# Latent attention layers of a four-layer decoder step: what the in-projection starts with moves into the out-projection ahead of it, and latent squares move from the heads stage into the in-projection

## The chip, the cores and the metric

The kernel runs as one launch on one core of a Trainium2 chip. The metric is the device time of one execution in microseconds (us), lower is better. The engines named below are TensorE (PE), VectorE (DVE), ScalarE (ACT), GpSimd (POOL) and SyncE (SP, which issues every DMA here).

## The reference, cut to what matters

Four layers, each `x <- x + W_out(mixer(in_proj(RMSNorm(x))) * silu(gate))`, on 1024 prompt tokens and 8 sample tokens (T = 1032 columns), width 1024. Layers 0 and 3 are latent attention (MLA), layer 1 is HGRN2, layer 2 is RG-LRU. The part of an MLA layer that the change touches:

```
h = rmsnorm(x, norm_g)
cq, ckv, kpe, gate = split(h @ w_in, [384, 640, 672])     # 384 + 256 + 32 + 512 columns
q   = rmsnorm(cq, g_ql) @ w_uq                            # needs the mean square of cq, of each token
ckv = rmsnorm(ckv, g_kv)                                  # needs the mean square of ckv
k_nope, v = split(ckv @ w_ukv)                            # then norms of q and k, rotary part, attention
```

## The kernel before, in words

Activations lie by feature: `c.x` is 128 partitions x 8 blocks (KD) x 1032 tokens, fp32. A projection is done at about fp32 precision as three products of the rounded type fp32r: weights and source are each split into a high part (ACT, a Copy that rounds) and a low part (a subtraction), and the products are hi x hi, hi x lo and lo x hi. One output block of 128 columns is 8 k-blocks x 3 products x 3 token tiles of 344 = 72 matmuls into three PSUM banks. Output blocks alternate between two sets of banks, two weight slots, and two slots each of parts (`w_hi`, `w_lo`). The order on each engine is written by hand; semaphores join the engines, and every stage (`Stage.block`) ends in a barrier of all engines.

`latent_projection` (the in-projection of an MLA layer, nine output blocks and then the narrow `kpe` block) does in this order:

- SP: in layer 0 the eight blocks of `x` and the weights; in layer 3 (`first` is False) `x` is already in place, so the weights alone. Then six small tables (`m.load`, `w_uq` among them), then a weight block whenever a slot is free.
- ACT: the table set for Ln and Exp, `src_hi` of eight blocks (L667), the high parts of weight blocks 0 and 1 (L656), squares of `x` (L659), and later `root()`: Ln and Exp of the sums of squares (L684, L687), which give `rstd`.
- POOL: the low parts of all weight blocks (L705). DVE: `src_lo` (L766), adding up the squares (L773), then `take(n)` (L777), which multiplies block n in PSUM by `rstd` into `m.z`.
- PE: block 0 (L729), each k-block as its `src_lo` comes; in layer 0 then the column sums of the squares (`sums()`, L740) and block 1, in layer 3 block 1 and then the sums; then blocks 2 to 8, each after `take` has emptied its banks.

`mla_heads` starts with squares of the two `ckv` blocks (ACT, L1060) and three `cq` blocks (L1062), a scaling of `w_uq` in place (L1065) and two additions on POOL (L937, L940). PE begins with the column sums of the `ckv` squares (L984), the first query product (L1010), sums of the `cq` squares (L1017) and a turn of `kpe` (L1021); then come, tile by tile of 128 tokens, keys (L1029), values, queries and transposes.

`output_projection` of the RG-LRU layer (layer 2) is `streamed_projection` with a `ring`: PE has blocks 0 and 1 nearly done before the stage starts (L226), the parts of the source are made by then, and blocks 2 to 7 follow (L382); DVE adds each to `c.x` (L461). It has no `norm_layer`, so ACT and POOL only split weights (L315, L351).

Of the kernel before, what the change touches and what calls it, by code (L numbers as in the profile page):

```python
# [66 lines left out]

class Chip:


    def __init__(self, nc, ctx, dram):
# [9 lines left out]
        self.parts = parts[:, :, 0, :], parts[:, :, 1, :]  # L81
        self.ident = sb("ident", [P, P])
# [147 lines left out]
def streamed_projection(c, w, blocks, kt, src, drain, norm_layer=None, early=None, x_back=None, x_in=None, x_out=None, ring=None, clear=False):  # L230
# [7 lines left out]
    with Stage(c, clear=clear) as st:  # L238
# [16 lines left out]
        if norm:  # L255
            norm.bank = base[0]
        block = st.block()
# [3 lines left out]
        def _(sp):  # L261
# [49 lines left out]
        def _(act):  # L311
# [20 lines left out]
            with act.Fori(2, pairs) as i:  # L332
                for u in range(2):
                    weight_hi(2 * i + u, u, 16 * i + (16 - 8 * ready))
                    square(2 * i + (u - 2), u)
            if blocks % 2:
                weight_hi(blocks - 1, 0, 16 * (pairs + 1))
            if norm:
# [9 lines left out]
        def _(pool):  # L348
# [4 lines left out]

            for m in range(ready, 4):
# [3 lines left out]
            with pool.Fori(2, pairs) as i:  # L358
                for u in range(2):
                    weight_lo(2 * i + u, u)  # L360
                    if norm:
                        norm.accumulate(pool, 2 * i + (u - 2), u)
            if blocks % 2:
                weight_lo(blocks - 1, 0)
            if norm:
                norm.accumulate(pool, blocks - 2, 0)

# [47 lines left out]
        def _(dve):  # L415
# [21 lines left out]
            if x_in is None:  # L437
# [21 lines left out]
def output_projection(c, w, kt, src, next_layer, x_back=None, x_in=None, x_out=None, ring=None, clear=False, early=None):  # L459
# [3 lines left out]
                        x_out=x_out, ring=ring, clear=clear, early=early)  # L463
# [127 lines left out]

def latent_projection(c, m, layer, j):
# [3 lines left out]
    with Stage(c) as st:  # L596
# [3 lines left out]
        src_hi = st.sb("src_hi", [P, KD, T], F32R)  # L600
        src_lo = st.sb("src_lo", [P, KD, T], F32R)
# [19 lines left out]
        drained = st.sem("block_drained")  # L621
        if first:
            c.decays.semaphores(st)
        block = st.block()
        pairs = blocks // 2
# [3 lines left out]
        def _(sp):  # L629
            if first:  # L630
                sp.dma_start(c.x[:, 0, :], dram["x"][:, 0, :]).then_inc(x_landed[0], 16)
                sp.dma_start(c.gains[:, :, :], dram["norm_g"]).then_inc(gains_landed, 16)
            sp.dma_start(ws[:, 0, :, :], w[0]).then_inc(w_landed[0], 16)
            for k in range(1, KD if first else 0):
                sp.dma_start(c.x[:, k, :], dram["x"][:, k, :]).then_inc(x_landed[k], 16)
            sp.dma_start(ws[:, 1, :, :], w[1]).then_inc(w_landed[1], 16)
# [6 lines left out]
            with sp.Fori(1, pairs) as i:  # L643
                for u in range(2):
                    sp.wait_ge(w_lo_done, 2 * i + (u - 1))
                    sp.dma_start(ws[:, u, :, :], w[bass.ds(2 * i + u, 1)].rearrange("a p k m -> p (a k) m")) \
                      .then_inc(w_landed[u], 16)
            sp.wait_ge(w_lo_done, blocks - 2)
            sp.dma_start(ws[:, 0, :, :], w[blocks - 1]).then_inc(w_landed[0], 16)

        @block.scalar
        def _(act):
            def weight_hi(n, u, landed_now):
                act.wait_ge(w_landed[u], landed_now)
                wait(act, summed, n - 1)
# [5 lines left out]
            load_ln_exp(nc)  # L661
            if first:
                act.wait_ge(gains_landed, 16)
            for k in range(KD):
# [4 lines left out]
                if k == 1:  # L669
# [2557 lines left out]
```

## Time and profile before

| | us |
|---|---|
| median of 3 runs (lowest, highest) | 2446.91 (2445.93, 2453.77) |
| the profiled execution, its own time | 2443.1 |
| its span, first to last instruction | 2441.3 |
| in-projection of layer 0 | 0 to 138.6 |
| heads stage of layer 0 | 138.6 to 237 |
| out-projection of the RG-LRU layer | 1655.7 to 1735.4 |
| in-projection of layer 3 | 1735.7 to 1867.6 |
| heads stage of layer 3 | from 1867.8 |

Times in the rows below are microseconds from the start of the span. PE is busy in 94% of the span, so the places to look at are those where it is not, and those where its clock is low: PEclk is the clock granted to it as a share of full speed (1.0 is 2.4 GHz, 0.5 is 1.2 GHz).

### The profile page before, as it was taken

The numbers are of one execution on the slowest core, as the hardware profiler recorded it, in microseconds if no ns is written. First come the engines' busy times: TensorE is split into PE (matmuls) and PEld (weight loads), VectorE is DVE, ScalarE is ACT, GpSimd is POOL, SyncE is SP. The second block draws the span as 40 slices with busy tenths as digits, with TensorE's granted clock in tenths as the row PEclk, the third lists the DMA queues.
The fourth block names the chain that finished last, engine by engine and source line by source line (L and its number), as shares of the span: only waits on it lengthen the run. The fifth ranks groups of instructions, "written<-read, shape, count | busy, mean of one in ns | idle before, by whom it ended". The sixth has DMA issues, their size and how long they took to land. (4 is left out here: it accounts for less than half of the span.)

```text
span 2441.3 us, 47634 instructions
## 1 busy us (share of the span) xinstructions
PE 2292.1 (94%) x17886; PEld 1901.0 (78%) x17886; DVE 1252.1 (51%) x1972; ACT 1097.7 (45%) x1873; POOL 722.9 (30%) x809
## 2 busy tenths in 40 slices
PE   7989999999889999999968989989899999999998
PEld 6956666666688999999968989989896566666668
DVE  5133555566443666766674166681412355655552
ACT  4055544555344544455552256661302655545541
POOL 2134322333030222332233325541211532322311
PEclk9999999999999999999979999999999999999999
DMA  4020434434331111111102111101213023434333
GB/s 151 26 75 1 122 107 114 112 95 120 121 130 45 49 51 55 40 50 54 46 28 106 35 53 49 40 20 52 70 35 117 28 83 108 119 102 112 110 105 139
DMA packets 104278, 187.62 MB, mean 77 GB/s; under 512 B 15722, under 2 KB 84332, under 8 KB 102916
## 3 DMA queue, kind: packets, MB, share of 16 engines
q1 hardware_dynamic: 104068, 184.81, 24.6%
q8 instruction: 133, 2.18, 0.4%
q14 instruction: 77, 0.63, 0.1%
HBM read 164.84 MB, written 19.92 MB: 76 GB/s over the span
## 5 line engine op out<-in xcount | busy, mean ns | idle before, releaser
L1507 POOL TENSOR_TENSOR latents_t_lo<-pages_t,latents_t_hi 128x256 fp32r<-128x256 f32 x256 | 187.7, 733 | 551.4 <-ACT latents_t_hi L1744 550.7
L1906 DVE TENSOR_REDUCE sums<-w_uq 128x8 f32<-128x512 f32 x256 | 175.2, 684 | 263.1 <-ACT w_uq L1752 262.8
L1752 ACT ACTIVATE w_uq<-ps 128x512 f32<-128x512 f32 x256 | 152.8, 597 | 209.6 <-PE ps L1592 208.8
L2209 PE MATMUL ps<-src_hi,w_hi 128*128 128x344 f32 x720 | 243.3, 338 | 2.8 <-ACT normed L2365 2.6
L1592 PE MATMUL ps<-w_uk_hi,latents_t_hi 128*128 128x512 f32 x512 | 236.1, 461 | 1.0 <-POOL latents_t_lo L1507 1.0
L2209 PE MATMUL ps<-src_hi,w_lo 128*128 128x344 f32 x720 | 233.5, 324 | 0.0
L2209 PE MATMUL ps<-src_lo,w_hi 128*128 128x344 f32 x720 | 233.4, 324 | 0.0
L1592 PE MATMUL ps<-w_uk_lo,latents_t_hi 128*128 128x512 f32 x512 | 203.7, 398 | 0.0
L1592 PE MATMUL ps<-w_uk_hi,latents_t_lo 128*128 128x512 f32 x512 | 203.3, 397 | 0.0
L1761 ACT ACTIVATE latents<-ps,bias,rq 128x256 f32<-128x256 f32 (+7 forms) x128 | 106.1, 829 | 131.3 <-DVE bias L1920 117.5
L1606 PE MATMUL ps<-residual,normed 96*128 96x512 f32 (+3 forms) x384 | 153.6, 509 | 8.8 <-ACT w_uq L1752 6.2
L2511 POOL TENSOR_TENSOR normed<-normed,k 128x512 f32<-128x512 f32 x56 | 96.8, 1730 | 201.4 <-ACT normed L2380 168.4
L2209 PEld LDWEIGHTS ps<-src_hi,w_hi 128*128 128x128 f32 x720 | 139.0, 193 | 7.2 <-ACT normed L2365 3.5
L461 DVE TENSOR_TENSOR residual<-ps,residual 128x1032 f32 (+1 forms) x30 | 37.0, 1233 | 206.8 <-PE ps L382 201.6
L2209 PEld LDWEIGHTS ps<-src_lo,w_hi 128*128 128x128 f32 x720 | 138.9, 193 | 0.5
L2209 PEld LDWEIGHTS ps<-src_hi,w_lo 128*128 128x128 f32 x720 | 138.4, 192 | 0.0
L1592 PEld LDWEIGHTS ps<-w_uk_hi,latents_t_hi 128*128 128x128 f32 x512 | 97.1, 190 | 45.4 <-issue 23.8
L2365 ACT ACTIVATE normed<-ps 128x344 f32<-128x344 f32 x96 | 43.0, 454 | 194.5 <-PE ps L2209 188.6
L729 PE MATMUL ps<-src_hi,w_hi 128*128 128x344 f32 x432 | 94.5, 328 | 29.8 <-POOL w_lo L705 22.4
L351 POOL TENSOR_TENSOR w_lo<-w_slots,w_hi 128x512 fp32r<-128x512 f32 (+1 forms) x24 | 44.2, 1844 | 242.4 <-ACT w_hi L315 242.4
L1592 PEld LDWEIGHTS ps<-w_uk_hi,latents_t_lo 128*128 128x128 f32 x512 | 96.9, 189 | 23.6
L1592 PEld LDWEIGHTS ps<-w_uk_lo,latents_t_hi 128*128 128x128 f32 x512 | 97.7, 191 | 18.9 <-issue 3.8
(368 smaller groups left out, 5582.3 us busy)
## 6 DMA issues: line engine op xcount, KB each, us to landing
pages_t<-in_pages_t SPq DMA_DIRECT2D x256, 208.0 KB, 2.6
pages<-in_pages SPq DMA_DIRECT2D x256, 128.0 KB, 2.1
w_slots<-in_w_hgrn SPq DMA_DIRECT2D x30, 512.0 KB, 3.6
w_slots<-in_w_mla_in SPq DMA_DIRECT2D x18, 512.0 KB, 3.7
x_home<-residual SPq DMA_DIRECT2D x2, 4128.0 KB, 14.5
w_slots<-in_w_rg SPq DMA_DIRECT2D x14, 512.0 KB, 3.5
residual<-in_x SPq DMA_DIRECT2D x8, 516.0 KB, 9.0
residual<-in_x SPq DMA_DIRECT2D x1, 4128.0 KB, 13.8
```

Of the source, the lines that this page charges most:

```text
L351: nc.gpsimd.tensor_tensor(w_lo[:, u, :, :], ws[:, u, :, :], w_hi[:, u, :, :].bitcast(F32), ALU.subtract).then_inc(w_lo_done, 1)
L461: streamed_projection(c, w, KD, kt, src, lambda m, psum: c.nc.vector.tensor_tensor(block_of(c.x, m), psum, block_of(c.x, m), ALU.add), nex ...
L729: mm = nc.tensor.matmul(c.ps[:, NT * u + t, 0:TT], a[:, u, k, :], b[:, k, cols], start=(k == 0 and p == 0), stop=(k == KD - 1 and p == 2))
L1507: nc.gpsimd.tensor_tensor(lat_lo[:, g % DEPTH, :, :].rearrange("p k t -> p (k t)"), ring[:, g % RING, 0:KVL], lat_hi[:, g % DEPTH, :, :].r ...
L1592: mm = nc.tensor.matmul(keys(g), x[:, e, k, :], y[:, k, :], start=(n == 0), stop=(n == len(products) - 1))
L1606: mm = nc.tensor.matmul(S[:, lo:hi], c.h[0:QK, 2 * f + e, qt * P:(qt + 1) * P], c.x[0:QK, 2 * f + e, lo:hi], start=True, stop=True)
L1752: nc.scalar.activation(sq[:, g % 2, :], keys(g), ACT.Square).then_inc(squared, 1)
L1761: nc.scalar.activation(probs[:, G % 2, e, 0:n], S[:, 0:n], ACT.Exp, scale=m.rq[:, qt, 2 * f + e:2 * f + e + 1], bias=bias[:, u:u + 1], acc ...
L1906: nc.vector.tensor_reduce(ss[:, b % 2, p, :], sq[:, g % 2, :].rearrange("p (h d) -> p h d", h=H), AX.X, ALU.add).then_inc(ssum, 1)
L2209: mm = nc.tensor.matmul(bank[:, 0:TT], w[:, slot, kk, :], x[:, kk, cols], start=(kk == 0 and m == 0), stop=(kk == KD - 1 and m == 2))
L2365: nc.scalar.activation(raw[:, place, t * TT:(t + 1) * TT], bank[:, 0:TT], ACT.Copy) \
L2511: nc.gpsimd.tensor_tensor(halves(z[:, l % 2, 0:SEQ], half)[:, :, 0, :], halves(dd[:, l % 2, 0:SEQ], half)[:, :, 0, :], halves(k[:, 0:SEQ], ...
```

## The change

Four edits.

1. In the RG-LRU out-projection (`carry`), ACT makes the high part of each block of the new `x` times the gain of layer 3, and its square; POOL adds the squares up; DVE makes the low part; all for blocks 0 to 6. The first weight block of layer 3 is loaded and split there too. The new buffer `carried_src` lies at the top of the on-chip memory; the rest uses free parts of `c.h`. ACT's, POOL's and DVE's loops are written out there.
2. `latent_projection` of layer 3 starts with block 0 at once (k-blocks 0 to 6 from what was carried), makes only block 7's parts and square, and does the sums right after block 0 in place of after block 1.
3. `latent_projection` of layer 0 sums blocks 0 and 1 together, k-block by k-block (`FIRST_TWO`), with the column sums after both. Loads come in another order, DVE makes the low parts of the first two weight blocks, `load_ln_exp` moves behind the squares, and the high part of weight block 2 stands behind `root()` and the high part of the `kpe` weights.
4. In both, ACT squares the latents (blocks 0 to 4) between weight blocks, POOL adds those of `cq`, ACT scales `w_uq`; `mla_heads` no longer does any of it. All engines' loops over blocks are written out.

```diff
 class Carried:            # in Chip: self.carried = Carried(self, parts)
+        self.hi, self.lo = src[:, 0, :, :], src[:, 1, :, :]     # carried_src [P, 2, KD, T], F32R
+        self.sums = c.h[:, 0, :]
+        self.squares = c.h[:, 1, :], c.h[:, 7, :]
 ...
 def streamed_projection(..., carry=None):                      # SP
+            if carry is not None:
+                sp.dma_start(cd.w, carry[1]).then_inc(w_next_landed, 16)
 ...                                                            # ACT, in square(m, u)
+                if carry is not None:
+                    act.wait_ge(drained, m + 1)
+                    nc.scalar.activation(cd.hi[:, m, :], c.x[:, m, :], ACT.Copy,
+                                         scale=c.gains[:, carry[0], m:m + 1]).then_inc(next_hi, 1)
+                    if m >= 2:
+                        act.wait_ge(next_added, m - 1)
+                    nc.scalar.activation(cd.squares[u], c.x[:, m, :], ACT.Square).then_inc(next_squared, 1)
 ...
+                for m in range(4, blocks):
+                    weight_hi(m, m % 2, 16 * (m // 2) + (16 - 8 * ready))
+                    square(m - 2, m % 2)
 ...
+            if carry is not None:
+                act.wait_ge(w_next_landed, 16)
+                nc.scalar.activation(cd.w_hi, cd.w, ACT.Copy).then_inc(w_next_hi, 1)
+                square(blocks - 2, 0)
 ...                                                            # DVE
+            if carry is not None:
+                one(0, 0)
+                one(1, 1)
+                for m in range(2, blocks):
+                    one(m, m % 2)
+                    next_low(m - 2)
+                next_low(blocks - 2)
 ...
 def latent_projection(c, m, layer, j):                         # SP
             if first:
-                sp.dma_start(c.x[:, 0, :], dram["x"][:, 0, :]).then_inc(x_landed[0], 16)
                 sp.dma_start(c.gains[:, :, :], dram["norm_g"]).then_inc(gains_landed, 16)
-            sp.dma_start(ws[:, 0, :, :], w[0]).then_inc(w_landed[0], 16)
+                sp.dma_start(ws[:, 0, :, :], w[0]).then_inc(w_landed[0], 16)
+                for k in range(2):
+                    sp.dma_start(c.x[:, k, :], dram["x"][:, k, :]).then_inc(x_landed[k], 16)
+            sp.dma_start(ws[:, 1, :, :], w[1]).then_inc(w_landed[1], 16)
+            if not first:
+                sp.dma_start(ws[:, 0, :, :], w[2]).then_inc(w_landed[0], 16)
 ...                                                            # ACT
             if first:
+                weight_hi(0)
+                act.wait_ge(gains_landed, 16)
+                for k in range(KD):
+                    high(k)
+                    if k == 1:
+                        weight_hi(1)
+                    square(k)
+                load_ln_exp(nc)
                 c.decays.exponentials(act)
                 root()
+                keys_hi()
+            else:
+                high(KD - 1)
+                square(KD - 1)
+                weight_hi(1)
+                load_ln_exp(nc)
                 root()
+                weight_hi(2)
+                keys_hi()
+            for n in range(2 + less, blocks):                  # less = 0 if first else 1
+                weight_hi(n)
+                if n >= 4:
+                    latent_square(n - 4)
+                if n - 4 == NQL - 1:
+                    for k in range(NQL):
+                        nc.scalar.activation(m.wuq[:, k, :], m.wuq[:, k, :], ACT.Copy, scale=m.gql[:, k:k + 1])
 ...                                                            # POOL
+            for n in range(2 if first else 1, blocks):
+                weight_lo(n)
 ...
+                if 5 <= n < 4 + NQL:
+                    add_latent_squares(n - 4)
 ...                                                            # PE
-            one(0, 0, head=True)
             if first:
+                for k, n in FIRST_TWO:      # (0,0) (1,0) (0,1) (1,1), then (k,0) (k,1) for k = 2 to 7
+                    pe.wait_ge(src_lo_done, k + 1)
+                    if k == 0:
+                        pe.wait_ge(w_lo_done, n + 1)
+                    mm = products(n, k, w_hi[:, n, :, :], w_lo[:, n, :, :])
 ...
                 sums()
-            one(1, 1, head=True)
-            if not first:
+            else:
+                for k in range(KD):
+                    if k == KD - 1:
+                        pe.wait_ge(src_lo_done, 1)
+                    mm = products(0, k, cd.w_hi, cd.w_lo)
+                mm.then_inc(summed, 1)
                 sums()
+                one(1)
+            for n in range(2, blocks):
+                one(n)
 ...                                                            # DVE
             if first:
+                weight_lo(0)
                 dve.wait_ge(gains_landed, 16)
+                for k in range(KD):
+                    low(k)
+                    if k == 1:
+                        weight_lo(1)
+                    if k:
+                        accumulate(k)
                 c.decays.compute(dve)
+            else:
+                low(KD - 1)
+                accumulate(KD - 1)
 ...
 def mla_heads(c, m, j, spill):                                 # PE
-            pe.wait_ge(kv_squared, NKV)
 ...
-            pe.wait_ge(wuq_scaled, NQL)
 ...
-                    pe.wait_ge(cq_added, 2)
 ...
 def rglru_layer(c, layer):
-        output_projection(c, c.dram["w_rg_out"], KD, out, None, ring=ring)
+        output_projection(c, c.dram["w_rg_out"], KD, out, None, ring=ring,
+                          carry=(layer + 1, c.dram["w_mla_in"][1][0]))
```

## Rows read from the trace of the kernel before

**Rows 1.** The page, busy time of the engines over the span.
```profile
PE 2292.1 (94%) x17886; PEld 1901.0 (78%) x17886; DVE 1252.1 (51%) x1972; ACT 1097.7 (45%) x1873; POOL 722.9 (30%) x809
```

**Rows 2.** Busy time by stretch, each after its length; then PEclk, DMA share, GB/s.
```profile
0.00:13.50 13.50, 0.02 (x1) 0.02 (x1) 4.27 (x3) 8.16 (x8) 2.72 (x5) 1.00 0.85 306
137.10:155.00 17.90, 12.60 (x52) 6.96 (x51) 4.00 (x4) 11.71 (x18) 5.65 (x4) 0.81 0.18 60
```

**Rows 3.** Timeline, in-projection of layer 3: start, us, engine line op [idle before].
```profile
1734.17 1.23 DVE L461 TENSOR_TENSOR residual<-ps,residual 128x1032 f32 x1 [10.12 <-PE ps L382]
1735.69 1.28 ACT L102 ACT_TABLE_LOAD   x1 [23.23 <-PEq L125]
1742.97 1.23 PE L729 MATMUL ps<-src_hi,w_hi 128*128 128x344 f32 x3 [8.95 <-POOL w_lo L705]
1756.48 0.64 PE L729 MATMUL ps<-src_hi,w_hi 128*128 128x344 f32 x3
1767.83 2.33 PE L740 MATMUL ps<-normed,ones 128*128 128x512 f32 x6
1770.63 1.06 ACT L687 ACTIVATE normed<-normed 128x1032 f32<-128x1032 f32 x1
1773.70 0.74 PE L729 MATMUL ps<-src_hi,w_hi 128*128 128x344 f32 x3 [3.53 <-DVE latents L777]
1786.98 1.24 DVE L777 TENSOR_TENSOR latents<-ps,normed 128x1032 f32 x1 [12.20 <-PE ps L729]
1798.34 1.23 DVE L777 TENSOR_TENSOR latents<-ps,normed 128x1032 f32 x1 [10.12 <-PE ps L729]
```

**Rows 4.** Timeline, in-projection of layer 0.
```profile
8.73 1.16 ACT L667 ACTIVATE src_hi<-residual,gains 128x1032 fp32r<-128x1032 f32 x1 [2.09 <-DMA residual<-in_x]
13.48 1.23 PE L729 MATMUL ps<-src_hi,w_hi 128*128 128x344 f32 x3 [13.48 <-POOL w_lo L705]
16.79 1.28 DVE L766 SCALAR_TENSOR_TENSOR src_lo<-residual,gains,src_hi 128x1032 fp32r<-128x1032 f32 x1
19.13 1.28 DVE L766 SCALAR_TENSOR_TENSOR src_lo<-residual,gains,src_hi 128x1032 fp32r<-128x1032 f32 x1
24.65 0.40 ACT L678 ACTIVATE w_kpe_hi<-w_kpe 128x256 fp32r<-128x256 f32 x1
37.69 2.40 POOL L705 TENSOR_TENSOR w_lo<-w_slots,w_hi 128x1024 fp32r<-128x1024 f32 x1 [7.53 <-ACT w_hi L656]
57.79 1.24 DVE L777 TENSOR_TENSOR latents<-ps,normed 128x1032 f32 x1 [10.14 <-PE ps L729]
```

**Rows 5.** Timeline, start of the two heads stages.
```profile
142.09 5.98 PE L984 MATMUL ps<-ckv_squares,ones 128*128 128x344 f32 x12 [4.98 <-ACT ckv_squares L1060]
1867.84 1.28 ACT L102 ACT_TABLE_LOAD   x1 [34.38 <-PEq L125]
1871.29 6.65 PE L984 MATMUL ps<-ckv_squares,ones 128*128 128x344 f32 x12 [4.98 <-ACT ckv_squares L1060]
```

**Rows 6.** Timeline, PE after shorter gaps, and a table load, in other stages.
```profile
652.75 0.66 PE L1629 MATMUL ps<-probs_t,values 128*64 128x128 f32 x8 [1.50 <-DVE probs_t L1928]
1439.73 5.43 PE L2833 MATMUL ps<-y,w_gates 128*128 128x344 f32 x12 [1.91 <-DVE y L2991]
1546.09 3.63 PE L2833 MATMUL ps<-y,w_gates 128*128 128x344 f32 x12
1548.10 1.28 ACT L2899 ACT_TABLE_LOAD   x1 [1.20 <-PE ps L2833]
```

**Rows 7.** Timeline, out-projection of the RG-LRU layer.
```profile
1659.27 1.06 ACT L315 ACTIVATE w_hi<-w_slots 128x1024 fp32r<-128x1024 f32 x1 [2.30 <-DMA w_slots<-in_w_rg_out]
1660.52 1.06 ACT L315 ACTIVATE w_hi<-w_slots 128x1024 fp32r<-128x1024 f32 x1 [0.19 <-DMA w_slots<-in_w_rg_out]
1662.80 1.23 PE L382 MATMUL ps<-src_hi,w_hi 128*128 128x344 f32 x3 [4.01 <-POOL w_lo L351]
1677.35 1.23 DVE L461 TENSOR_TENSOR residual<-ps,residual 128x1032 f32 x1 [17.17 <-PE ps L382]
```

More of the change, by code:

```diff
@@ L81, in __init__ @@
         self.parts = parts[:, :, 0, :], parts[:, :, 1, :]
+        self.carried = Carried(self, parts)
         self.ident = sb("ident", [P, P])
@@ L357, in _ @@
                 norm.accumulate_first(pool)
[L358 to L362, printed above, removed]
+            if carry is not None:
+                pool.wait_ge(next_squared, 2)
+                nc.gpsimd.tensor_tensor(cd.sums, cd.squares[0], cd.squares[1], ALU.add).then_inc(next_added, 1)
+            if carry is not None:
+                for m in range(4, blocks):
+                    weight_lo(m, m % 2)
+                    add_squares(m - 2, m % 2)
+            else:
+                with pool.Fori(2, pairs) as i:
+                    for u in range(2):
+                        weight_lo(2 * i + u, u)
+                        if norm:
+                            norm.accumulate(pool, 2 * i + (u - 2), u)
             if blocks % 2:
@@ L599, in latent_projection @@
         w_lo = st.sb("w_lo", [P, 2, KD, P], F32R)
-        src_hi = st.sb("src_hi", [P, KD, T], F32R)
-        src_lo = st.sb("src_lo", [P, KD, T], F32R)
+        cd = c.carried
+        src_hi, src_lo = cd.hi, cd.lo
         wk_hi = st.sb("w_kpe_hi", [P, KD, ROPE], F32R)
@@ L624, in latent_projection @@
         block = st.block()
-        pairs = blocks // 2
+        less = 0 if first else 1
         SUMS = [(6, slice(0, 512)), (7, slice(512, SEQ)), (6, slice(SEQ, T))]
@@ L659, in square, with high @@
                 nc.scalar.activation(sq[:, k, :], c.x[:, k, :], ACT.Square).then_inc(squared, 1)
[L661 to L664, printed above, removed]
+            def high(k):
                 if first:
@@ L718, in _, with products @@
         @block.tensor
         def _(pe):
-            def one(n, u, head=False):
-                pe.wait_ge(w_lo_done, n + 1)
-                if not head:
+            def products(n, k, a_hi, a_lo):
+                for p, (a, b) in enumerate(((a_hi, src_hi), (a_hi, src_lo), (a_lo, src_hi))):
+                    for t, cols in tiles():
+                        mm = nc.tensor.matmul(c.ps[:, NT * (n % 2) + t, 0:TT], a[:, k, :], b[:, k, cols],
+                                              start=(k == 0 and p == 0), stop=(k == KD - 1 and p == 2))
+                return mm
@@ L723, in one @@
+            def one(n):
+                u = n % 2
+                pe.wait_ge(w_lo_done, n + 1 - less)
+                if n >= 2:
                     pe.wait_ge(drained, n - 1)
                 for k in range(KD):
-                    if head and u == 0:
-                        pe.wait_ge(src_lo_done, k + 1)
-                    for p, (a, b) in enumerate(((w_hi, src_hi), (w_hi, src_lo), (w_lo, src_hi))):
-                        for t, cols in tiles():
-                            mm = nc.tensor.matmul(c.ps[:, NT * u + t, 0:TT], a[:, u, k, :], b[:, k, cols],
-                                                  start=(k == 0 and p == 0), stop=(k == KD - 1 and p == 2))
+                    mm = products(n, k, w_hi[:, u, :, :], w_lo[:, u, :, :])
@@ L780, in _ @@
             if first:
+                weight_lo(0)
                 dve.wait_ge(gains_landed, 16)
[L782 to L788 removed]
+                for k in range(KD):
[4 more added lines that the diff above has]
+                        accumulate(k)
                 c.decays.compute(dve)
+            else:
+                low(KD - 1)
+                accumulate(KD - 1)
             dve.wait_ge(rstd_ready, 1)
[L791 to L794 removed]
+            for n in range(blocks):
+                take(n)
             dve.wait_ge(summed, blocks + 1)
@@ L2005, in mla_layer @@
         x_home = c.dram["x"] if layer == 0 else c.dram["x_home"]
+        m.squares = [c.h[:, n, :] for n in (5, 6, 7, 3, 4)]
         latent_projection(c, m, layer, j)
```

166 lines of the change are left out of this document (80 added, 86 removed).

## The prediction

> **What bounds the kernel now.** Read first the busy time of the engines: PE works in 94% of the span, no other engine in much over half [rows 1]. So what can be won are the places where PE stands still or runs at its low clock. Next, the timeline around the two in-projections, by what PE waits for. In layer 3 [rows 3] the last sum of the out-projection is taken at 1734.17, the stage begins at 1735.7, and PE starts at 1742.97, after 8.95 us without work: a weight block had to land, be split by ACT and again by POOL. Its first 72 matmuls then take 13.51 us (to 1756.48) where a block at full clock takes 11.36 (1786.98 to 1798.34). After block 1 and the sums it stands again for 3.53 us, until the first `take` has emptied a bank, since the sums came so late. Block 2, from 1773.70 to 1786.98, took 13.3 us, so the clock had dropped once more. In layer 0 [rows 4] PE first works at 13.48, and block 2 is done at 57.79. Third, the starts of the heads stages [rows 5]: PE's first work, the sums of the `ckv` squares, waits 4.98 us for ACT's squares, and the twelve instructions then take 5.98 and 6.65 us. The same twelve of the same shape take 3.63 elsewhere [rows 6], so here too the clock was low; over that start of layer 0 the granted clock was 0.81 of the full 2.4 GHz [rows 2]. From there the stage is PE's.
>
> **Layer 3's in-projection.** Removed: the wait for the weight block's landing and its two splits, and seven of eight source blocks. What replaces it, step by step, in times of before.
> DVE's queue in the out-projection ends with `one(7)`, `next_low(5)`, `next_low(6)`, so two instructions of 1.28 us (a `src_lo` row [rows 4]) stand behind the last sum: the barrier moves back from 1735.7 by 2.4 to 1738.1. POOL is done by then, so nothing slows them. PE starts at 1738.15. Block 7's parts need ACT's 1.16 and DVE's 1.28 [rows 4], done near 1740.7, long before PE comes to k-block 7. PE has stood 4.1 us, so I charge a low clock at the start: the cases seen are 13.51 - 11.36 = 2.15 [rows 3], 13.28 - 0.1 - 11.36 = 1.8 (block 2, the 0.1 being the step from PE's end to DVE) [rows 3], and 1662.80 to 1677.35 less the same, 3.1, after a gap of 4.01 [rows 7]. I take 2.1, bounds 1.8 and 3.1. Block 0 ends at 1738.15 + 11.36 + 2.1 = 1751.6; the sums take 2.33 [rows 3], to 1753.9; `rstd` is there 3.9 us after the sums begin (1767.83 to 1770.63 + 1.06 [rows 3]), at 1755.5, while PE is on block 1, so the wait of 3.53 us goes: block 1 to 1765.3, block 2 to 1776.7, its `take` at 1776.8. Before: 1786.98. **Gain 10.2**, bounds 9.2 and 10.5. What is late next there is nothing: ACT's and POOL's parts of weight block 2 follow `rstd` and end near 1760, five us before need.
> The added work in the out-projection is hidden: per block ACT gets 1.16 and about as much for a square, POOL one addition, DVE 1.28, where each is idle some 9 of 11.36 us (DVE waits 10.12 before its sum [rows 3]). Of the start one edit could reach the path: the third 512 KB load beside the two whose landing ACT waits for [rows 7]. It is queued behind them, and these two landed one after the other, 1.25 us apart, so I take 0; bound, if the three share evenly and all land with the last, 2 x 1.25 = 2.5.
>
> **Layer 0's in-projection.** The weights go second in the queue; a block issued at a stage's start is there 3.6 us later (table load 1.28 and 2.30 idle before the split at 1659.27 [rows 7]), so about 4.8 for one issued near 1.2. ACT splits it first. Whether that first Copy now needs a table load of its own, since `load_ln_exp` went behind, no row shows; a load stands between the wait and the instruction that needs it [rows 6], so I take one, 1.28, bound 0. ACT: load to 6.1, split (1.06 [rows 7]) to 7.2, `src_hi(0)` (1.16) to 8.3; DVE: the weights' low part (at most the 1.28 of a `src_lo`) to 8.5, `src_lo(0)` to 9.8. PE starts at 9.8 in place of 13.48; if the weights land 1 us later, 1 later. After that PE isn't short of input: it spends 2 x 11.36 / 8 = 2.84 per k-block, DVE makes one in 2.34 (16.79 to 19.13 [rows 4]), block 1 of `x` lands as before at 8.7 (the same bytes lie ahead of it), and POOL, which had slowed DVE, has nothing to do. Both blocks end at 9.8 + 22.7 + 2.1 = 34.6.
> Then comes the price. Weight block 2 is split only after `root()` and the `kpe` weights: sums to `rstd` 3.9, `kpe` 0.40, split 1.06, POOL 2.40 [rows 3, 4, 7], so PE starts block 2 at 42.4 and has stood about 5 us: 2.1 more for the clock. Its `take` is at 42.4 + 11.36 + 2.1 + 0.1 = 56.0, before it was 57.79. **Gain 1.8**. Bounds: start 1 later or 0.9 earlier, each of the two cold starts 0.3 less or 1.0 more, POOL 1.0 more if DVE's `take` holds it up: -2.2 and 3.3.
> The Trainium skill (ScalarE: Activation LUTs, What ACT_TABLE_LOAD costs) adds a drain of 1.38 us to a load's 1.28; by it layer 0 would gain 0.4 and the sum below be 22.8. The row of a load agrees with the 1.28 [rows 6]; no row here shows the drain, so I leave it out.
>
> **The heads stages.** The squares, the additions and the scaling of `w_uq` now lie between ACT's weight splits, which are some 11 us apart (two `take`s: 1786.98, 1798.34 [rows 3]), behind each split in ACT's queue, so no split gets later; the last square needs block 4 only. PE can begin with the stage, at +0.05 in place of +3.45 (1867.84 to 1871.29 [rows 5]): 3.4 each. The gap before it falls from 4.98 to about 1.6 us. Was the clock kept after such gaps? After 1.50 us eight matmuls took 0.66, at the full clock; after 1.91 the twelve took 5.43 [rows 6]. 1.6 is nearer the first, so I take 3.63 in place of 5.98 and 6.65: 2.35 and 3.0 more. Bounds: 3.63 and 6.65. The steps that follow (query product, `cq` sums, turns, then the factors) hang on PE's order alone and all move along. **Gain 3.4 + 2.35 + 3.4 + 3.0 = 12.2**, bounds 6.1 and 12.2.
>
> **Sum.** 10.2 + 1.8 + 12.2 = 24.2. The profiled execution took 2443.1 us, span 2441.3, so 2418.9 by it. It lies 3.8 below the median of the runs, 2446.91; carried to the median: 2422.7.
>
> **Rivals.**
> *The clock falls in the heads all the same.* For it: 5.43 us after a gap of only 1.91 [rows 6], and a start that always was slow [rows 5]. Then only 3.4 each: gain 18.8, time 2428.1. Chance 0.24.
> *The third load in the out-projection delays the first two.* Gain 24.2 - 2.5 = 21.7, time 2425.2. Against: the one-by-one landing [rows 7]. 0.08.
> *The heads don't start earlier in effect*, because another chain holds the first key product: Ln, Exp and two scalings of `ckv`. With sums done 3.7 us into the stage, about 1.1 + 1.1 + 2.5 more make 8.4 (estimates by size from the ACT and DVE rows of 1032 columns [rows 3, 4]), and PE has a product of 4 and smaller sums to do meanwhile, so hardly. Gain 12.0, time 2434.9. 0.06.
> *Slower.* PE's loop over blocks 2 to 8 is written out in both layers, 14 blocks of 72 matmuls. If PE can't be fed with straight-line instructions as fast as from a loop, each block gets longer: 24.2 / 14 = 1.7 us a block takes all of the gain, from 2.25 the kernel is measurably slower, and 3 us a block gives 2446.9 - 24.2 + 42 = 2464.7. Against it: block 1 of layer 3 is written out already and took 1767.83 - 1756.48 = 11.35 [rows 3]. 0.08, mostly near no change.
>
> **How the numbers follow.** Forecast 0.52, more gain than its bounds 0.02, the rest as given. Bounds added up, lowest -2.2 + 9.2 + 6.1 - 2.5 = 10.6, highest 3.3 + 10.5 + 12.2 = 26.0, so 2420.9 to 2436.3 at the median; below it I allow for the profiled time being the truer zero (3.8, and a little for the runs): 2415 to 2437. That leaves out the last rival and little else. 0.3% is 7.3 us, about what a measurement of this kernel tells from no change: faster 0.92, same 0.05 and slower 0.03, both from the last rival.
>
> **What the profile after would show.** Right: PE starts at about 10 and at 2.5 us after the last sum of the out-projection; no wait of PE for `take` in layer 3; block 2 of layer 0 done near 56 with some 5 us of idle PE ahead of it; the `ckv` sums first in the heads, in 3.6 us. Wrong: these sums at 5.4 or more, out-projection blocks later than before, blocks of more than 11.4 us in the written-out part, or in layer 0 a gap so long that its term turns negative.

## The result and the profile after

The changed kernel takes 2436.51 us (median of 12 runs, 2430.36 to 2443.12), the kernel before on the same chips 2454.86 us (12 runs, 2445.93 to 2460.43). The ratio is 0.9934, 95% interval [0.9918, 0.995]: faster by more than 0.3%, by 16 us as a ratio and 18.35 us as a difference of medians. The forecast was 2422.7 us, a gain of 24.2. The time lies at the upper end of the range, 2437.

The places that the prediction spoke of went nearly as it said. The timeline of the kernel after in layer 0's in-projection, the answer to [rows 4] (start, us, engine, line, then idle time before and what ended it):

```profile
0.76 1.28 ACT L733 ACT_TABLE_LOAD   x1 [0.76 <-PEq L3304]
5.03 1.06 ACT L733 ACTIVATE w_hi<-w_slots 128x1024 fp32r<-128x1024 f32 x1 [2.98 <-DMA w_slots<-in_w_mla_in]
9.04 2.09 PE L818 MATMUL ps<-carried_src,w_hi 128*128 128x344 f32 x6 [9.04 <-DVE carried_src L873]
...
33.97 2.25 PE L838 MATMUL ps<-normed,ones 128*128 128x512 f32 x6
...
41.55 0.65 PE L818 MATMUL ps<-carried_src,w_hi 128*128 128x344 f32 x1 [5.34 <-POOL w_lo L795]
...
54.55 1.23 DVE L891 TENSOR_TENSOR latents<-ps,normed 128x1032 f32<-128x1032 f32 x1 [13.85 <-PE ps L818]
```

PE starts 4.4 us earlier, stands 5.34 us before block 2, and that block's `take` comes at 54.55 where it came at 57.79. The same view around layer 3's in-projection, the answer to [rows 3]:

```profile
1737.14 0.62 PE L440 MATMUL ps<-src_hi,w_lo 128*128 128x344 f32 x3
1737.80 1.23 DVE L532 TENSOR_TENSOR residual<-ps,residual 128x1032 f32<-128x1032 f32 x1 [8.92 <-PE ps L440]
1738.95 2.49 DVE L497 SCALAR_TENSOR_TENSOR carried_src<-residual,gains,carried_src 128x1032 fp32r<-128x1032 f32 x2
...
1741.74 4.64 PE L818 MATMUL ps<-carried_src,gate_parts 128*128 128x344 f32 x15 [3.98 <-PEq L142]
...
1755.93 2.19 PE L838 MATMUL ps<-normed,ones 128*128 128x512 f32 x6
...
1758.72 1.07 ACT L752 ACTIVATE normed<-normed 128x1032 f32<-128x1032 f32 x1
...
1780.98 1.23 DVE L891 TENSOR_TENSOR latents<-ps,normed 128x1032 f32<-128x1032 f32 x1 [10.13 <-PE ps L818]
```

From the last sum of the out-projection to block 2's `take` it is 43.18 us (1737.80 to 1780.98), before 52.81 (1734.17 to 1786.98): 9.6 us less. PE's wait for `take` is gone. And the start of the two heads stages, the answer to [rows 5]:

```profile
135.56 3.71 PE L1089 MATMUL ps<-normed,ones 128*128 128x344 f32 x12 [1.57 <-PEq L142]
...
146.25 0.60 PE L1132 MATMUL ps<-w_uk,latents 128*8 128x512 f32 x1 [0.37 <-ACT r L1175]
...
1861.98 3.71 PE L1089 MATMUL ps<-normed,ones 128*128 128x344 f32 x12 [1.56 <-PEq L142]
...
1872.67 0.60 PE L1132 MATMUL ps<-w_uk,latents 128*8 128x512 f32 x1 [0.38 <-ACT r L1175]
```

The twelve sums begin 0.04 us into the stage and take 3.71 us in both layers, at full clock. The first key product, with which the old order of work goes on, comes at 146.25 and 1872.67. In the kernel before, the last matmuls of the RG-LRU out-projection and the two first key products stand here:

```profile
155.06 0.60 PE L1029 MATMUL ps<-w_uk,latents 128*8 128x512 f32 x1 [0.38 <-ACT r L1079]
...
1733.40 0.62 PE L382 MATMUL ps<-src_hi,w_lo 128*128 128x344 f32 x3
...
1884.93 1.02 PE L1029 MATMUL ps<-w_uk,latents 128*8 128x512 f32 x1
```

So measure what the edits touched by two lengths: from the span's start to the first key product of layer 0, 155.1 before and 146.2 after, 8.8 less by unrounded times; and from the last matmuls of the RG-LRU out-projection (1733.40, 1737.14) to the first key product of layer 3, 151.5 and 135.5, 16.0 less. Together 24.8 us less, and 24.2 was forecast. Its parts, cut at block 2's `take`, are 9.7 (from those matmuls) and 6.3 in layer 3 and 3.2 and 5.6 in layer 0. Yet this profiled execution took 2442.26 us, hardly less than the 2443.1 of before. It lost the gain where no instruction was changed. These are the windows (length, busy time of PE, PEld, DVE, ACT and POOL, then PEclk, DMA share, GB/s) of the two attention stages in the kernel before, cut into the body, the tail (from the last wide score product, 96x512, to the first pieces of the out-projection) and those pieces, which PE does ahead of its stage; layer 0, then layer 3:

```profile
237.90:642.80 404.90, 394.02 (x2892) 266.64 (x2892) 237.25 (x543) 201.81 (x463) 121.83 (x259) 0.99 0.39 107
642.80:660.00 17.20, 15.15 (x150) 10.53 (x150) 6.83 (x23) 3.67 (x9) 0.00 (x0) 1.00 0.61 247
660.00:666.70 6.70, 6.41 (x40) 6.15 (x40) 2.18 (x4) 0.66 (x2) 0.00 (x0) 1.00 0.00 0
1967.30:2373.60 406.30, 395.78 (x2892) 268.21 (x2892) 237.39 (x543) 201.82 (x463) 121.84 (x259) 0.99 0.38 107
2373.60:2390.80 17.20, 15.15 (x151) 10.53 (x150) 6.81 (x23) 3.67 (x9) 0.00 (x0) 1.00 0.61 247
2390.80:2397.50 6.70, 6.40 (x41) 6.15 (x40) 2.18 (x4) 0.68 (x2) 0.00 (x0) 1.00 0.00 0
```

And the tails and pieces of the kernel after:

```profile
635.40:660.50 25.10, 23.15 (x151) 16.10 (x150) 6.89 (x23) 3.67 (x9) 0.00 (x0) 0.64 0.43 170
660.50:669.60 9.10, 8.80 (x41) 8.54 (x40) 2.18 (x4) 0.71 (x2) 0.00 (x0) 0.71 0.00 0
...
2362.50:2387.60 25.10, 23.16 (x151) 16.09 (x150) 6.88 (x23) 3.67 (x9) 0.00 (x0) 0.64 0.42 169
2387.60:2396.70 9.10, 8.80 (x41) 8.54 (x40) 2.17 (x4) 0.70 (x2) 0.00 (x0) 0.71 0.01 2
```

The same instructions, the same DVE and ACT time, but PEclk 0.64 and 0.71 in place of 1.00: mostly 1.2 GHz. Each layer loses 7.9 + 2.4 = 10.3 us, 20.6 in all. The two bodies together take 2.1 us more than before, and the HGRN layer (PE's first matmul there to its first in the out-projection's stage) takes 600.7 in place of 599.3. So 24.1 of the 24.8 us are accounted for as lost outside the edited stages.

### The profile page after: what moved, and what is told of

It is laid out like the page before. It is cut to its first block and busy times, and to the rows that moved or that the text cites. A ratio compares the mean times of both kernels' runs of the same rounds, so it can differ in the third digit from the quotient of the medians.

```text
span 2440.5 us, 47435 instructions
## 1 busy us (share of the span) xinstructions
PE 2310.5 (95%) x17886; PEld 1917.6 (79%) x17886; DVE 1234.9 (51%) x1968; ACT 1098.5 (45%) x1874; POOL 730.6 (30%) x813
## 5 line engine op out<-in xcount | busy, mean ns | idle before, releaser
L2306 PE MATMUL ps<-src_hi,w_hi 128*128 128x344 f32 x720 | 243.5, 338 | 2.9 <-ACT normed L2462 2.6
L818 PE MATMUL ps<-carried_src,w_hi 128*128 128x344 f32 x816 | 154.0, 325 | 14.4 <-DVE carried_src L873 9.0
L818 PEld LDWEIGHTS ps<-carried_src,w_hi 128*128 128x128 f32 x816 | 135.9, 192 | 14.5 <-DVE carried_src L873 9.0
L532 DVE TENSOR_TENSOR residual<-ps,residual 128x1032 f32<-128x1032 f32 (+1 forms) x30 | 37.0, 1233 | 205.2 <-PE ps L440 200.0
L1688 PEld LDWEIGHTS ps<-w_uk_hi,latents_t_lo 128*128 128x128 f32 x512 | 97.3, 190 | 23.9
## 6 DMA issues: line engine op xcount, KB each, us to landing
x_home<-residual SPq DMA_DIRECT2D x2, 4128.0 KB, 15.2
```

Source lines behind the costliest of these rows:

```text
L818: mm = nc.tensor.matmul(c.ps[:, NT * (n % 2) + t, 0:TT], a[:, k, :], b[:, k, cols], start=(k == 0 and p == 0), stop=(k == KD - 1 and p == 2))
L1688: mm = nc.tensor.matmul(keys(g), x[:, e, k, :], y[:, k, :], start=(n == 0), stop=(n == len(products) - 1))
L2306: mm = nc.tensor.matmul(bank[:, 0:TT], w[:, slot, kk, :], x[:, kk, cols], start=(kk == 0 and m == 0), stop=(kk == KD - 1 and m == 2))
```

## The experiments

Three theories. T1: the clock falls in these tails in some executions of either kernel, whatever the edits. T2: the edits bring it down. T3: the clock is one budget, so what is kept here is lost elsewhere. In the table every kernel has its ratio to the kernel before, measured beside it, and tail + pieces of its profiled execution.

| kernel | ratio [95%] | layer 0 | layer 3 |
|---|---|---|---|
| before | 1 | 17.2 + 6.7 | 17.2 + 6.7 |
| again_before | 0.9995 [0.9971, 1.0018] | 25.1 + 9.2 | 17.2 + 6.7 |
| after | 0.9934 [0.9918, 0.995] | 25.1 + 9.1 | 25.1 + 9.1 |
| again_after | 0.9926 [0.9899, 0.9952] | 20.4 + 8.2 | 25.1 + 9.1 |
| only_heads (edit 4) | 0.9943 [0.9923, 0.9963] | 21.4 + 6.7 | 17.2 + 6.7 |
| only_layer3 (edits 1, 2) | 0.9947 [0.9928, 0.9965] | 25.1 + 9.2 | 17.2 + 6.7 |
| only_layer0 (edit 3) | 0.9962 [0.9938, 0.9986] | 17.2 + 6.7 | 17.2 + 6.7 |
| kept_before | 0.9981 [0.9964, 0.9998] | 17.2 + 6.7 | 17.2 + 6.7 |
| kept_after | 0.9891 [0.9858, 0.9925] | 17.2 + 8.2 | 17.2 + 8.2 |
| fill_layer0 | 0.9917 [0.9896, 0.9937] | 17.2 + 6.7 | 21.7 + 6.7 |
| fill_layer3 | 0.9899 [0.9873, 0.9924] | 25.1 + 9.2 | 17.2 + 8.2 |
| layer3_heads (1, 2, 4) | 0.9955 [0.9933, 0.9977] | 21.4 + 6.7 | 25.1 + 9.1 |
| layer0_heads (3, 4) | 0.9926 [0.9902, 0.9949] | 17.2 + 6.7 | 17.2 + 6.7 |
| layer0_layer3 (1, 2, 3) | 0.9941 [0.9918, 0.9965] | 17.2 + 6.7 | 17.2 + 6.7 |
| later_1 | 0.996 [0.9943, 0.9977] | 17.2 + 6.7 | 20.4 + 8.2 |
| later_2 | 0.9967 [0.9945, 0.9988] | 20.5 + 8.2 | 21.6 + 6.7 |
| later_3 | 0.9949 [0.9927, 0.9972] | 25.1 + 9.2 | 20.4 + 8.2 |
| both_fixes | 0.9892 [0.9859, 0.9926] | 25.1 + 9.1 | 19.8 + 6.7 |
| fixes_kept | 0.9842 [0.9819, 0.9865] | 17.2 + 6.7 | 17.2 + 6.7 |

**Both kernels once more**, with no edit.

> The kernel before once more, for a second profile of it. Theory 1 (clock): from the last wide scores of an attention stage to the first products of the out-projection behind them PE's clock falls or does not from one execution to the next, in both kernels; the profiled before had it high in both layers (17.2 us each), the profiled after low in both (25.1 each). Then this profile may show 25 in one or both of its stretches, and its time lies above 2443.1 by some 8 for each. Theory 2 (the edits make that stretch slow): 17 in both again. Either way the ratio to before is 1.000.

> The changed kernel once more. Theory 1: the in-projections and heads are faster by the same 3.2, 5.6, 9.7 and 6.4 us as in its first profile, and the two attention tails take 17 or 25 as it happens. Theory 2: 25 in both again. The ratio should come out near 0.993 once more.

The second profiled execution of the kernel before took 2459.26 us, 16 more than the first. Its HGRN layer takes 603.2 us in place of 599.3, and its layer 0 shows (body, tail, pieces) what the kernel after showed:

```profile
237.95:644.38 406.43, 396.02 (x2891) 268.03 (x2891) 237.24 (x543) 201.76 (x463) 121.85 (x259) 0.99 0.38 107
644.38:669.46 25.08, 23.13 (x151) 16.02 (x150) 6.88 (x23) 3.67 (x9) 0.00 (x0) 0.64 0.43 169
669.46:678.64 9.18, 8.88 (x40) 8.63 (x40) 2.17 (x4) 0.67 (x2) 0.00 (x0) 0.70 0.00 0
```

So in layer 0 the fall needs no edit, and the execution behind the prediction was one without it. The executions that were not profiled spread in the same way, by their mean granted clock: those of again_before go from 2443.52 us at 0.968 to 2461.87 at 0.960, those of the kernel after from 2430.36 at 0.966 to 2443.12 at 0.961. By an estimate from its profile, 2442.26 - 20.6 = 2421.7 would be the kernel after with both tails whole; the fastest of its 18 executions took 2430.36. Where the fall begins is seen in PE's timeline ahead of the tail. First the kernel before, first execution:

```profile
638.87 0.66 PE L1533 MATMUL ps<-ident,scores_t 128*128 128x128 f32 x4 [2.09 <-ACT scores_t L1721]
639.36 1.04 PE L1617 MATMUL ps<-ident,latents 128*128 128x128 f32 x8
641.56 0.27 PE L1538 MATMUL ps<-ident,max 128*8 128x128 f32 x1 [1.16 <-DVE max L1846]
642.46 0.38 PE L1542 MATMUL ps<-diag,ones 8*128 8x8 f32 x2 [0.62 <-DVE diag L1852]
642.77 1.98 PE L1606 MATMUL ps<-residual,normed 96*128 96x512 f32 x4
```

Then the same kernel in the second execution:

```profile
640.03 0.66 PE L1533 MATMUL ps<-ident,scores_t 128*128 128x128 f32 x4 [2.09 <-ACT scores_t L1721]
640.52 1.60 PE L1617 MATMUL ps<-ident,latents 128*128 128x128 f32 x8
...
644.38 3.78 PE L1606 MATMUL ps<-residual,normed 96*128 96x512 f32 x4
```

PE waits three times on the last sample's softmax, in the first execution 2.09, 1.16 and 0.62 us, with short matmuls between. After the same wait of 2.09 us the eight `latents` matmuls took 1.04 us once and 1.60 the other time, and the four wide ones 1.98 and 3.78: the clock had fallen within the eight. The Trainium skill (TensorE: Matmul & The Clock Gate, What's actually happening) says that the activity monitor runs free and doesn't begin anew with a kernel, so that one program can differ between runs; the two executions agree with that for layer 0. (For layer 3 the runs further down don't look like it.)

**One edit alone.** Made from the kernel after by putting back the functions of before for the other edits:

```
 only_heads:  latent_projection and streamed_projection as before,
              but ACT squares the latents between weight blocks; mla_heads of after
 only_layer3: layer 0's latent_projection and mla_heads as before
 only_layer0: layer 3's latent_projection, the out-projection and mla_heads as before
```

> The latent squares and the scaling of w_uq in the in-projection alone (edit 4), the in-projections in their old order. By the stages: 5.6 us in layer 0 and 6.4 in layer 3, as PE starts with the stage and the sums of the ckv squares take 3.6 in place of 6.0 and 6.7. Theory 1: whole time 12 faster than before at equal clocks in the tails, and the tails 17 or 25 as it happens. Theory 2, if this edit is what slows the tails: 25 in both, no gain or a loss.

> What is carried from the out-projection into layer 3 alone (edits 1 and 2). By the stages: 9.7 us in the in-projection of layer 3, nothing in the heads and nothing in layer 0. Theory 1: layer 0 as before but for the clock of its tail. Theory 2, if these edits slow the tails: 25 us in the tail of layer 3 and 17 in that of layer 0, whose code ahead of it is unchanged.

> The new start of layer 0 alone (edit 3). By the stages 3.2 us, as in the changed kernel, nothing elsewhere. Theory 1: tails 17 or 25 as it happens, so between 3 us faster and nothing that can be told. Theory 2, if this edit slows the tails: both at 25.

By the two lengths, only_heads gains 6.5 + 6.1 = 12.6 us, only_layer3 0.2 + 10.0, only_layer0 3.3 + 0.1: the terms add up, to 26.3, so the stages leave no shortfall for an interaction to explain. The ratios give 14, 13 and 9 us, each within 5 or 6, together 36, more than twice what all edits give at once (16). The 9 us of only_layer0 are a miss: at most 3 were expected. The stages gain the same either way, so the shortfall of the whole lies outside them. None of the three has the tails that theory 2 forecast for it (only_layer3 has layer 3's whole and layer 0's low).

**The clock held in both tails.** The waits ahead of the tail get extra matmuls of 512 columns into a bank that is overwritten unread: 20 in each layer, the results unchanged.

```diff
+            def fill(count):
+                for _ in range(count):
+                    nc.tensor.matmul(KEYS[:, :], m.wuk_hi[:, 0, 0:P], m.wuk_hi[:, 0, :], start=True, stop=True)
                 def turn_scores():
+                    if b == NS - 1:
+                        pe.wait_ge(squared, NS * PAGES)
+                        fill(8)
                     pe.wait_ge(sct_taken, b + 1)
                 def turn_max():
+                    if b == NS - 1: fill(4)
                 def spread_max():
+                    if b == NS - 1: fill(2)
 ...
+                if G == NG_: fill(6)
                 weighs(0)
```

> The kernel before, with PE kept at work in the last sample's chain of each attention tail: 8, 4 and 2 matmuls of 512 columns ahead of three waits there and 6 ahead of a fourth; their products are overwritten unread. Theory 1 (the clock falls in the tail by chance, because PE stands there): both tails take 17 to 18 us, out-projection pieces behind them 6.7, in every execution, and the median falls by about 8 (one tail of two on average) to some 2443. Theory 2 (the edits slow the tail): no change against before but for a little extra work. Theory 3 (the clock falls ahead of the filled places, or because of what PE does and not because it stands): tails of 20 to 25 us remain.

> The changed kernel with the same filling. Theory 1: both tails 17 to 18 us, the median near 2421, and 22 to 25 us under the kernel before with the same filling: the whole of the gain that the stages show. Theory 2: the tails stay at 25 and the time at 2437. Theory 3: in between.

The timeline of kept_after at that place; L1626 is the filling:

```profile
629.02 2.10 PE L1626 MATMUL ps<-w_uk_hi 128*128 128x512 f32 x8
631.18 0.66 PE L1636 MATMUL ps<-ident,scores_t 128*128 128x128 f32 x4
631.67 1.04 PE L1724 MATMUL ps<-ident,latents 128*128 128x128 f32 x8
...
635.10 1.98 PE L1713 MATMUL ps<-residual,normed 96*128 96x512 f32 x4
```

All tails of the filled layers, in every kernel that has the filling, took 17.2 us. By the ratios the kernel after gains 0.43% by it (0.9934 to 0.9891, 10.5 us) and the kernel before 0.19% (4.7 us); by the quotients of the medians, 0.9925 to 0.9886 and 1 to 0.9961, it is 9.5 and 9.6 us, the same for both. Half of kept_before's ten executions lie at 2442.5 to 2443.1 us, the time of the kernel before with both tails whole. With both filled the change is worth 0.9891 / 0.9981 = 0.9910, 22 us of 2450, and the medians, 2443.85 and 2425.64, differ by 18.2, where theory 1 expected 22 to 25. The intervals don't tell 18 from 24.8. The profile of kept_after shows clock lost elsewhere: against kept_before 1.5 us in the pieces of each layer, 3.7 over the HGRN layer, 2.4 in the out-projection of layer 2. Those 9.1 us are about what the two profiled executions, 16.3 us apart, lack of the 24.8.

**The filling in one layer alone** (`if b == NS - 1 and j == 0`, or `j == 1`).

> The kernel after, with the filling matmuls in the attention tail of layer 0 alone. T1 (each tail loses its clock by itself, and each lost tail costs some 8 us and 2.4 us in the out-projection's first pieces): layer 0's tail at 17.2 us, layer 3's as in the kernel after at 20 to 25; half of what filling both gave, so a ratio near 0.9912, about 2431 us. T3 (it is one clock budget for the whole kernel, the tails only where it shows): the filling here costs it elsewhere and the ratio stays at 0.993.

> The kernel after, with the filling matmuls in the attention tail of layer 3 alone. T1: layer 3's tail at 17.2 us, layer 0's at 20 to 25, ratio near 0.9912, about 2431 us, and fill_layer0 and fill_layer3 together give what filling both gave. T2 (the edits themselves make layer 3's tail slow, and only that one): this alone gives nearly all, 0.989, and fill_layer0 nothing, 0.993.

The two tails and pieces of fill_layer0, filled in layer 0, then not in layer 3:

```profile
635.00:652.24 17.24, 16.58 (x156) 11.58 (x155) 6.81 (x23) 3.67 (x9) 0.00 (x0) 1.00 0.62 247
652.24:658.95 6.71, 6.42 (x40) 6.16 (x40) 2.18 (x4) 0.67 (x2) 0.00 (x0) 1.00 0.00 0
2351.79:2373.44 21.65, 19.59 (x150) 12.87 (x150) 6.89 (x23) 3.67 (x9) 0.00 (x0) 0.78 0.48 196
2373.44:2380.15 6.71, 6.41 (x40) 6.16 (x40) 2.18 (x4) 0.67 (x2) 0.00 (x0) 1.00 0.01 2
```

Layer 0 alone gives 0.17% (4 us), layer 3 alone 0.35% (9 us), both 0.43%. In the profiles each tail answers to its own filling. In the times layer 3's filling pays, barely beyond the noise, which speaks against T3's one budget in its strict form, by which nothing can be won; layer 0's 4 us are within the noise, so T2's "layer 3 only" isn't excluded by them. That clock kept in the tails is in part lost elsewhere, as in kept_after's profile, stays open.

**Two edits of three.** Without filling, layer 3's tail was low in the profile of each kernel with the whole change and in none of those with one edit or none; that hardly is T1's chance. Three kernels leave out one part each.

> Edits 1, 2 and 4, without edit 3 (layer 0's in-projection as before). By stages 9.7 + 12 = 21.7 us less. If the fall in layer 3's attention tail belongs to these edits together (layer 3 is then the same code as in the kernel after): layer 3's tail at 20 to 25 us in the profile, ratio near 0.9945. If it comes by chance, or belongs to the whole change with its shift in time: 17.2 us in this profile is as well possible, ratio near 0.991.

> Edits 3 and 4, without 1 and 2. By stages 3.2 + 12 = 15.2 us less, ratio 0.9938 if no tail loses its clock more often than in the kernel before. If the fall in layer 3's tail belongs to edits 1, 2 and 4 together: layer 3's tail at 17.2 us here. If it belongs to any shift in time: it can be at 20 to 25 here too.

> Edits 1, 2 and 3, without 4 (the heads stages as before). By stages 9.7 + 3.2 = 12.9 us less, ratio 0.9947 if no tail loses its clock more often than in the kernel before. If the fall in layer 3's tail belongs to edits 1, 2 and 4 together: layer 3's tail at 17.2 us here. If it belongs to any shift in time: it can be at 20 to 25 here too.

Tail and pieces of layer 3, first in layer3_heads:

```profile
2361.38:2386.46 25.08, 23.12 (x150) 16.05 (x149) 6.88 (x23) 3.67 (x9) 0.00 (x0) 0.64 0.42 169
2386.46:2395.58 9.12, 8.82 (x40) 8.56 (x40) 2.18 (x4) 0.67 (x2) 0.00 (x0) 0.71 0.00 0
```

and in layer0_heads:

```profile
2358.22:2375.45 17.23, 15.18 (x151) 10.56 (x150) 6.82 (x23) 3.67 (x9) 0.00 (x0) 1.00 0.62 246
2375.45:2382.16 6.71, 6.41 (x41) 6.16 (x40) 2.17 (x4) 0.67 (x2) 0.00 (x0) 1.00 0.00 0
```

It falls with edits 1, 2 and 4 together and with neither 4 nor 1 and 2 alone. The times agree: layer3_heads, with 21.7 us less work, gains 11 us (0.9955), layer0_heads with 15.2 less gains 18. The full change (0.9934) is no better than layer0_heads (0.9926), within the intervals: about what edits 1 and 2 win in layer 3's in-projection is gone in its tail.

**Layer 3 moved in time.** The same twelve sums are done two, three and four times in layer 3, which moves the rest of it by 3.4, 7.0 and 10.4 us (first key product 138.9, 142.5 and 145.9 us after the out-projection, in place of 135.5).

```diff
+            for again in range(1 + (1 if j == 1 else 0)):      # 2 and 3 in later_2, later_3
                 for k in range(NKV):
                     for t, cols in tiles():
```

> The kernel after, with the twelve sums of the ckv squares done twice in layer 3 (the same results into the same bank, 3.6 us of PE work more), so that all that follows in layer 3 comes some 3.6 us later and nothing else changes. If the tail of layer 3 falls because of when it comes: 17.2 and 6.7 us in one at least of the three kernels with one, two and three repeats, and there 10.3 us less than the kernel after, less the 3.6 us a repeat. If it falls because of what the edits' code does in layer 3: 25.1 and 9.1 us in all three, each repeat 3.6 us slower, this one near 0.995.

> The same with the sums done three times, some 7.3 us later. By time: layer 3's heads then start nearly where those of the kernel with edits 1, 2 and 3 alone have their first key product (141.6 us after the out-projection against 135.5), whose tail took 17.2 us, so 17.2 here and a ratio near 0.992. By code: 25.1 us, near 0.9965.

> The same with the sums done four times, some 11 us later, nearly where the kernels without edits 1 and 2 have the first key product (145.1), whose tails took 17.2 us. By time: 17.2 here and a ratio near 0.9935. By code: 25.1 us, near 0.998.

Neither expectation held. The tail recovered in none of the three, but it was not the full 25.1 + 9.1 either: 28.6, 28.3 and 28.6 us with the pieces, between 23.9 and 34.2. Moved to where the kernels without the edits have it, layer 3 still lost clock, so its distance from the out-projection alone doesn't decide. Why edits 1, 2 and 4 together bring it on, and no part of them, stays open.

**What the edits left over.** Two waits that the timelines above still show: in the out-projection the low parts of blocks 5 and 6 stand behind the last sum, and in layer 0 the split of weight block 2 stands behind `root()`.

```diff
-                for m in range(2, blocks):
+                for m in range(2, blocks - 1):
                     one(m, m % 2)
                     next_low(m - 2)
+                next_low(blocks - 3)
                 next_low(blocks - 2)
+                one(blocks - 1, (blocks - 1) % 2)
 ...
                 c.decays.exponentials(act)
+                weight_hi(2)
                 root()
 ...
-            for n in range(2 + less, blocks):
+            for n in range(3, blocks):
```

> The changed kernel with two instructions moved: in the out-projection DVE makes the low parts of blocks 5 and 6 ahead of the last sum, and in layer 0 ACT splits weight block 2 ahead of the root. By the stages: the barrier 2.4 us earlier and PE's gap there 1.7 in place of 4.1, so perhaps no low clock at the start of layer 3 (1.5 to 2 more); in layer 0 block 2 starts when the first take is done, about 2 earlier. So 4 to 7 us in these two stages; the whole time 2431 to 2434, or less where the clock of the tails is kind.

> Both further edits (the low parts of blocks 5 and 6 ahead of the last sum, the high part of weight block 2 ahead of the root in layer 0) together with the filling matmuls in both attention tails. Theory T1 (the tails' clock is a cost of its own, apart from the edits): the edits' 2.7 and 5.1 us, read as stage lengths, add to what kept_after showed, 0.9891, so 0.9891 - 7.8 / 2453 = 0.986, about 2418 us; both tails 17.2 us. Rival (filling and the two edits win the same time, so both_fixes' 0.9892 already holds it): 0.989, about 2426. Third (clock lost in the tails turns up in another stage when it is kept there): stages of the HGRN layer or the out-projection longer by up to 5 us, 0.988.

The timeline of fixes_kept at layer 3's start:

```profile
1725.04 1.23 DVE L534 TENSOR_TENSOR residual<-ps,residual 128x1032 f32<-128x1032 f32 x1 [4.35 <-PE ps L440]
...
1726.59 11.61 PE L821 MATMUL ps<-carried_src,gate_parts 128*128 128x344 f32 x72 [1.59 <-PEq L142]
```

PE stands 1.59 us in place of 3.98, and its 72 matmuls then take 11.61 us in place of 14.2 (1741.74 to the sums at 1755.93): the shorter wait pays twice, 2.4 us of waiting and 2.6 of clock. The length to the first keys falls from 135.5 to 130.4. In both_fixes, without the filling, the wait and the 72 matmuls are the same. Layer 0's fix gave 2.6 us in both_fixes (146.2 to 143.7) but 0.5 in fixes_kept (145.8), where block 2 began later (40.05, in both_fixes 38.83) and lost more clock. The times are better than forecast: both_fixes has 2425.96 us where 2431 to 2434 was expected, some 10 us less than the kernel after by the ratios, of which the two lengths show 7.7.

fixes_kept takes 2412.31 us (2410.72 to 2415.04), ratio 0.9842 [0.9819, 0.9865], the fastest of all. T1's 0.986 lies within the interval, the 0.989 and 0.988 of the two others don't. Both its tails are whole, as those of the first execution of before were, so these two can be compared without the clock of the tails: 2443.1 - 2412.3 = 30.8 us. The two lengths give 9.3 + 21.1 = 30.4 of it; less the fixes' 0.5 and 5.1, some 25 us are the change itself.

## Why the prediction was right and wrong

- **Layer 3's in-projection**, 10.2: 9.6. The start after the last sum was right to 0.04 us (3.94, forecast 3.98; the 2.5 in the list of signs fits the end of that sum, 2.7). The cold first block cost 14.2 - 11.36 = 2.8 where 2.1 was taken, inside the bounds.
- **Layer 0's in-projection**, 1.8: 3.2. The step that failed is the table load between the wait and the first Copy: it ran at 0.76, while the weights were still on their way, and cost nothing. PE started at 9.04, not 9.8. The two blocks with their cold start took 24.9 (forecast 24.8), the gap before block 2 was 5.34 (about 5), and that block lost 1.5 to the clock, not 2.1.
- By an estimate with the Trainium skill's drain (ScalarE: Activation LUTs, What ACT_TABLE_LOAD costs) the term would have been 0.4. The load lay ahead of the path, so this start doesn't test the drain. Other rows of the kernel before do: 57 of its 73 table loads have less than 0.05 us of idle ACT on either side. One of 1.28 us starts at 843.70, right behind an ACTIVATE, and the next ACTIVATE starts at 844.99. No drain of 1.38 us is seen there.
- **The heads**, 12.2: 11.8. The sums start with the stage and run at full clock, and the first key products come that much earlier, so the rival by which the heads don't start earlier in effect is refuted.
- **The rivals.** "The clock falls in the heads" forecast a gain of 18.8, and the medians differ by 18.35. The mechanism is still refuted: 3.71 us in both layers. Only the size fits. The third load is refuted too: ahead of block 2 of the out-projection PE stands 4.01 us before and 3.96 after, and from its first matmul of that stage to its last ones it takes 77.7 and 77.6 us. So is the written-out loop: a block takes 10.13 + 1.23 = 11.36 from `take` to `take`, as before.
- **The sum**, 24.2: 24.8 in the stages, 16 to 18 in the time. The step that failed is "carried to the median: 2422.7". It holds everything outside the edited stages fixed, at what one execution showed, and no rival speaks of it. That execution had both attention tails at full clock, and its 2443.1 us lies 11.8 below the median of 12 runs. The changed kernel has layer 3's tail low in every unfilled profile, 10.3 us where all of it falls. In the profiled executions this is shown: 20.6 of the 24.8 us went in the tails and the pieces behind them, 3.5 in the bodies and the HGRN layer. With both tails whole, in fixes_kept against the first execution of before, the gain of the stages arrives in the time (30.4 and 30.8).
- That the tails also make up the 24.2 - 18.35 = 5.85 us that the medians lack is not shown. By the ratios the filling gives the kernel after 5.8 us more than the kernel before, by the medians nothing more, and with both filled the medians differ by 18.2 still. Clock lost in other stages is as likely a part of it.
- The 2436.51 lies 13.8 above the forecast: 5.85 from the smaller gain, and 7.95 because the median shown for the kernel before, 2446.91 of 3 runs, was that far below the 2454.86 of 12.

## What to carry to other kernels

Before summing gains on a profile, look for stretches where PE waits often between short matmuls while the clock is still high: there a gain won elsewhere can be lost again, and one profiled execution can't tell how often. When stages got faster and the time did not, compare the granted clock of the untouched stages first, in two executions of the same kernel. Where such a stretch exists, harmless matmuls in its waits are a cheap trial, and a shorter wait ahead of a dense stage can be worth twice its length.

## What was not expected of the hardware

- The same program, same instructions, lost its clock in layer 0's tail in one execution and not in another: PEclk 1.00 and 0.64, 10.3 us.
- In layer 3 that was no chance: all eight unfilled profiles with edits 1, 2 and 4 show it, whole or in part, and none of the seven others.
- Twenty matmuls in waits of PE, whose products nobody reads, make the kernel after faster, by 10.5 us as a ratio and 9.5 by the medians. With the two fixes its runs lie within 4.3 us (5 runs), those of the kernel after within 12.8 (12 runs); but both_fixes, without the filling, has 4.6 (4 runs), so the filling isn't shown to be what makes them alike.
